# Routing weights also scattered to a table in DRAM, from GpSimd, inside an encoder kernel

## The reference

```python
q = (xc @ wq).reshape(C, PEER_HEADS, 2, half)                 # 8 heads, two halves of 128
s = jnp.einsum('thpd,hpkd->thpk', q, subkeys)                 # 128 keys a side
sv, si = lax.top_k(s, PEER_TOPK)                              # 16 best of each side
cand = sv[:, :, 0, :, None] + sv[:, :, 1, None, :]            # 16 x 16 sums
cid = si[:, :, 0, :, None] * PEER_NKEYS + si[:, :, 1, None, :]
fs, fi = lax.top_k(cand, PEER_TOPK)                           # 16 experts a head
g = jax.nn.softmax(fs, axis=-1)
a = jax.nn.gelu(jnp.einsum('tc,thkc->thk', xc, u_tab[eid]))
out = jnp.einsum('thk,thkc->tc', g * a, v_tab[eid])
```

## Time and profile before

| | |
|---|---|
| timed runs | 2017.39, 2022.19 and 2021.06 us, median 2021.06 |
| profiled execution | span 2017.2 us; the page gives no other time for it |
| TensorE busy | 2008.9 us (100% of the span), granted clock 0.9 to 1.0 of full in all slices |
| GpSimd (POOL) busy | 1603.3 us (79%) |
| VectorE (DVE) busy | 1298.3 us (64%) |
| ScalarE (ACT) busy | 1118.2 us (55%) |
| DMA | 358.41 MB, 178 GB/s on average |

### The profile page before, as it was taken

One profiled execution on the slowest core, in us unless ns is written; L12 is line 12 of the kernel. 1 busy time (PEld: TensorE's weight loads), 2 busy tenths in 40 slices (PEclk: granted clock), 3 DMA queues, 4 the chain that ended last, 5 costly groups with the idle time before them and its releaser, 6 DMA issues.

```text
span 2017.2 us, 42413 instructions
## 1 busy us (share of the span) xinstructions
PE 2008.9 (100%) x12436; PEld 1745.7 (87%) x12436; DVE 1298.3 (64%) x2815; ACT 1118.2 (55%) x2453; POOL 1603.3 (79%) x1316
## 2 busy tenths in 40 slices
PE   9999999999999999999999999999999999999999
PEld 8989888888888888888888898888888888888887
DVE  6787599888887333333378865998888873333333
ACT  6565666654444555555565556556544455555554
POOL 7777879987777888888877677998877778888886
PEclk9999999999999999999999999999999999999999
DMA  9444645544444555555584455555544445555554
GB/s 278 166 145 147 209 162 190 187 169 148 154 146 147 196 190 195 194 191 194 191 244 151 135 178 177 178 185 180 167 155 147 153 149 197 189 196 190 195 193 150
DMA packets 103396, 358.41 MB, mean 178 GB/s; under 512 B 11744, under 2 KB 16802, under 8 KB 103076
## 3 DMA queue, kind: packets, MB, share of 16 engines
q1 hardware_dynamic: 102900, 355.41, 53.0%
q10 hardware_dynamic: 432, 2.18, 0.3%
HBM read 356.49 MB, written 1.05 MB: 177 GB/s over the span
## 4 chain that ended last, share of the span: by engine, by line
PE 71%; POOL 15%; issue 11%; POOLq 0%; ACT 0%; DMA 0%; SPq 0%; DVE 0%; DVEq 0%; ACTq 0%
PE bank L1975 34%; PE bank L1621 21%; POOL w_lo L438 15%; PE bank L1623 10%; PE bank L1914 4%; PE bank L1594 0%; PE bank L1598 0%; PE bank L1596 0%; PE bank L1893 0%; DMA ring<-stream 0%; POOLq L436 0%; POOLq L459 0%; ACT w_hi L501 0%; SPq L403 0%; PE bank L2001 0%
## 5 line engine op out<-in xcount | busy, mean ns | idle before, releaser
L438 POOL TENSOR_TENSOR w_lo<-ring,w_hi 128x512 fp32r<-128x512 f32 x1048 | 1401.4, 1353 | 323.6 <-ACT w_hi L501 322.7
L501 ACT ACTIVATE w_hi<-ring 128x512 fp32r<-128x512 f32 x1312 | 752.5, 620 | 185.4 <-PE bank L1598 131.6
L1621 PE MATMUL bank<-act_parts,w_hi 128*128 128x512 f32 x2048 | 722.8, 398 | 0.4 <-POOL w_lo L438 0.2
L1623 PE MATMUL bank<-act_parts,w_lo 128*128 128x256 f32 x2048 | 569.8, 278 | 0.0
L438 DVE TENSOR_TENSOR w_lo<-ring,w_hi 128x512 fp32r<-128x512 f32 x256 | 236.7, 925 | 450.0 <-ACT w_hi L501 449.8
L1621 PEld LDWEIGHTS bank<-act_parts,w_hi 128*128 128x128 f32 x2048 | 384.2, 188 | 88.9 <-POOL w_lo L438 0.9
L1975 PE MATMUL bank<-w_hi,e_hi 128*128 128x512 f32 x1024 | 398.9, 390 | 0.2
L1975 PE MATMUL bank<-w_hi,e_lo 128*128 128x512 f32 x1024 | 398.4, 389 | 0.0
L1975 PE MATMUL bank<-w_lo,e_hi 128*128 128x512 f32 x1024 | 398.4, 389 | 0.0
L1623 PEld LDWEIGHTS bank<-act_parts,w_lo 128*128 128x128 f32 x2048 | 385.4, 188 | 0.0
L837 ACT ACTIVATE e_hi<-arena 128x256 fp32r (+1 forms) x256 | 106.8, 418 | 316.0 <-PE bank L1975 316.0
(11 more groups left out here) (245 smaller groups left out, 2533.2 us busy)
## 6 DMA issues: line engine op xcount, KB each, us to landing
ring<-stream SPq DMA_DIRECT2D x654, 512.0 KB, 3.3
arena<-rpb_in SPq DMA_DIRECT2D x8, 512.0 KB, 7.3
arena<-dft_in SPq DMA_DIRECT2D x4, 512.0 KB, 5.0
arena<-subkeys ACTq DMA_DIRECT2D x2, 1024.0 KB, 5.7
ring<-stream SPq DMA_DIRECT2D x4, 256.0 KB, 5.4
xT<-x_in SPq DMA_DIRECT2D x4, 256.0 KB, 5.6
arena<-w_in SPq DMA_DIRECT2D x2, 512.0 KB
arena<-decay_in SPq DMA_DIRECT2D x2, 512.0 KB
```

The lines of the kernel that those rows point to most:

```text
L438: eng.tensor_tensor(w_lo[:, part_, :], ring[:, tile % RING, half * HT:(half + 1) * HT], w_hi[:, part_, :].bitcast(F32), ALU.subtract).then ...
L501: nc.scalar.activation(w_hi[:, 2 * (tile % AHEAD) + half, :], ring[:, tile % RING, half * HT:(half + 1) * HT], ACT.Copy).then_inc(hi_ready ...
L1621: T.matmul(out_[:, 0:2 * S], weights(w_hi, tile, k), both[:, :, k, :], start=(k == 0), stop=False, skip_group_check=True)
L1623: ins = T.matmul(out_[:, 0:S], weights(w_lo, tile, k), both[:, 0, k, :], start=False, stop=(k == KT - 1), skip_group_check=True)
```

## The change

Only the second layer is touched. VectorE, right after `route_done`, computes for the first 128 tokens the place of each slot's weight in a table (token + 256 x (i + 128 x j), by the code below), and copies the weights to a tile of their own; then it signals `places_made`. GpSimd's loop of that layer ends at tile 163. Its last 36 tiles below 200 (164 to 199, which are u_tab's tiles 92 to 127) are written out one by one, and behind the low halves of each even one an indirect DMA writes one slot: 128 weights of 4 bytes, one per partition, each to its own place in a table of 16.8 MB in DRAM. These are 18 DMAs, of slots 0 to 17. GpSimd waits for `places_made` before tile 164, and for the 18 landings at the end of the program. Nothing reads the table. (The constant SPREAD_TILES is not used.)

```diff
+SPREAD_AT = 92
+        token_col = sb("token_col", [P, 1])
+        place_u = sb("place_u", [P, PH * TOPK], U32)
+        weight_u = sb("weight_u", [P, PH * TOPK])
+        weights_out = nc.dram_tensor("weights_out", (NK * NK * S, 1), F32, kind="Internal").ap()
...
-                with pool.Fori(1, POOL_TILES // RING) as i:
+                first_turns = POOL_TILES // RING if l == 0 else (T_U + SPREAD_AT) // RING
+                with pool.Fori(1, first_turns) as i:
                     for s in range(RING):
                         low_parts(pool, l, i, s)
+                if l:
+                    pool.wait_ge(places_made, 1)
+                    for n in range(T_U + SPREAD_AT, POOL_TILES):
+                        low_parts(pool, l, 0, n)
+                        if n % 2 == 0:
+                            slot = (n - T_U - SPREAD_AT) // 2
+                            pool.indirect_dma_start(
+                                weights_out, bass.IndirectOffsetOnAxis(ap=place_u[:, slot:slot + 1], axis=0),
+                                weight_u[:, slot:slot + 1], None).then_inc(spread_out, 16)
...
             for l in range(DEPTH):
                 pool_layer(l)
+            pool.wait_ge(spread_out, 16 * ((NK - SPREAD_AT) // 2))
...
+                def spread_places():
+
+                    flat = top_if[:, :, :, :].rearrange("p a b c -> p (a b c)")[:, 0:PH * TOPK]
+                    rest_ps = bank[6][:, 3 * P:4 * P]
+                    link(V.tensor_tensor(rest_ps, identity, iota[:, :], ALU.mult))
+                    link(V.tensor_reduce(token_col[:, :], rest_ps, AX, ALU.add))
+                    link(V.scalar_tensor_tensor(flat, slots[:, 0, 1, :], float(NK), slots[:, 0, 0, :],
+                                                ALU.mult, ALU.add))
+                    link(V.tensor_scalar(flat, flat, float(S), token_col[:, 0:1], ALU.mult, ALU.add))
+                    V.tensor_copy(weight_u[:, :], slots[:, 0, 2, :])
+                    V.tensor_copy(place_u[:, :], flat).then_inc(places_made, 1)
...
                 V.drain().then_inc(route_done.sem, 1)
+                if l:
+                    spread_places()
                 worked(80, ROUTED)
```

More of the change, by code:

```diff
@@ L61 @@
 LATE = NK - ROUTED
+SPREAD_AT = 92
+SPREAD_TILES = 32
 C_G1, C_G2, C_GB, C_QG, C_KG, C_CW, C_CB = 0, 8, 16, 32, 33, 34, 70
@@ L320, in encoder_kernel @@
         route_done = sig("route_done", 1)
+        places_made = sem("places_made")
+        spread_out = sem("spread_out")
         onehot_j_made = sig("onehot_j_made", TGROUPS)
```

## The result

Over 18 executions each on the same chip the kernel before took 2020.93 us (2017.39 to 2025.05) and the changed one 2028.88 us (2024.51 to 2030.55). The ratio is 1.0039, 95% interval 1.0033 to 1.0045: 6.7 to 9.1 us more. The forecast was 2026. The time lies in its range, also just inside the narrow one of the likeliest case (2020 to 2029), but the class with most chance (within 0.3%) did not come: the change costs 0.39%.

The account below looks back on a forecast made before the run. TensorE was taken to bound the kernel. VectorE's lateness (4.0 us) plus the last DMA (1.1) made 5.1 us on the median of 2021.06, so 2026 us (+0.25%), range 2019 to 2045.

Parts of the forecast that it names:

- the likeliest case: Whole kernel: DMAs hidden, VectorE's lateness costs TensorE 4 us; chance 0.50, taken alone 2020 to 2029 us.
- the class with most chance: Whole kernel: time within 0.3% of the kernel before (6.1 us, up to 2027.1); chance 0.51.
- TensorE bounds, and the DMAs are hidden by GpSimd's rest: Layer 2's late tiles: 17 DMAs of 1.3 us each cost nothing; two-tile turns stay at TensorE's 7.00 us.
- The room of 1.9 us a turn: Layer 2's late tiles: GpSimd rests 0.23 + 1.68 us per two-tile turn, so a DMA up to 1.9 fits.
- Rival A: Layer 2's late tiles: a DMA holds GpSimd over 1.9 us, making it the bound; 2038 to 2124 us, chance 0.28.
- The last DMA costs 1.1: Behind tile 126, GpSimd runs without rest, so the last DMA delays TensorE by 1.1 us.
- VectorE's instructions wait for the end of GpSimd's instruction: Behind route_done: VectorE's six new instructions with SBUF operands wait for GpSimd's halves; the next sum starts 4.8 us late.
- rival B: Behind route_done: VectorE's waits don't bite, sum 2.9 us late, TensorE loses 2.1; 2024 us, chance 0.12.
- TensorE loses 4.0 of it: First late tiles of layer 2: VectorE's 4.8 us lateness less 0.8 of room costs TensorE 4.0 us, once.
- the room was 1.1, not 0.8: Before the 24 small matmuls near 1440: group 3's one-hots were put 0.83 us ahead of TensorE's need.
- Packets: Layer 2's stream: 2304 small packets must triple a ring refill's 3.2 us landing before ScalarE waits; no cost.
- Code loading (C): First DMA on GpSimd loads code: 0.7 us more, 2027 us, or 5.4 more, 2031.5, by the skill; chance 0.07.

Follow-up runs that it names:

- e7: Changed kernel with new tensors last, places computed in VectorE's earlier rest, weights copied by ScalarE, DMAs behind tiles 88 to 122: 2016.73 us, 0.9998.
- e6: Changed kernel with new tensors last and VectorE's six new instructions replaced by eight, none with both sides in SBUF: 2020.32 us, 1.0012.
- e5: Changed kernel with its three new SBUF tensors allocated behind all others, so no old one moves: 2021.21 us, 1.0019.
- e4: Kernel before with the three new SBUF tensors allocated ahead of the one-hots (shifted 1028 bytes), used by nobody: 2023.47 us, 1.0027.
- e10: Kernel before with unused place_u and weight_u in front of the one-hots (shifted 1024 bytes): 2020.47 us, 0.9999.
- e11: Kernel before with unused token_col alone in front of the one-hots (shifted 4 bytes): 2025.21 us, 1.0030.
- e1: Changed kernel without the DMAs and with GpSimd's loop as before; VectorE's six instructions and the three tensors stay: 2028.43 us, 1.0052.
- e8: Changed kernel with tensors last, places and weights from constants, two DMAs behind each even tile (36): 2027.98 us, 1.0044.
- e9: Changed kernel with tensors last, places and weights from constants, three DMAs behind each even tile (54): 2052.92 us, 1.0171.
- e0: Kernel before, with no edit, timed against itself and profiled a second time: 2019.80 us, 1.0005.

## Why the prediction was right or wrong

- **TensorE bounds, and the DMAs are hidden by GpSimd's rest**: right. The turn of layer 2's late stretch is 7.00 us with them. One DMA was put at 1.3 us; with its rest it is 1.15. The room of 1.9 us a turn is confirmed from the other side: 1.15 fits and 2.43 lengthens the turn by 0.46. Rival A (0.28) did not occur; 0.75 us more on each DMA would have made it true.
- **The last DMA costs 1.1**: 0.9 measured, seen as idle in front of tile 127 in all kernels that have it there, and gone in e7.
- **VectorE's instructions wait for the end of GpSimd's instruction**: right, and rival B wrong. Waiting were the place (0.94 us), the scaling by 256 (1.36) and the copy of the weights (1.23); the casting and the reduction were short, as forecast. So three were at 0.8 us or more, where four were forecast. The first product took only 0.48 because it started 0.34 before GpSimd's half ended. In sum 4.5 late, forecast 4.8. With one side in PSUM the same lengths are 0.28 to 0.34 (e6). The Trainium skill's page "SBUF — State Buffer", section "Who interferes with whom", gives two SBUF inputs and the two-port modes as what locks; the rows agree, the copy with a single input included.
- **TensorE loses 4.0 of it**: 3.4 measured, or 2.9 if only what the rows show is counted. The step was right in kind and in place (between 1430 and 1441, behind ScalarE's gelus L844 and L868, which stand behind VectorE's late sums); the room was 1.1, not 0.8. e5 shows this step and the one before alone: +3.8 us, forecast 5.1.
- **Packets**: the 2304 small packets of the prediction are 576 by the profile, and the stream's tiles land in 3.3 us as before.
- **Code loading (C)**: the first DMA took 1.10 us, 0.12 more than the others. It did not occur; the 6 us of the Trainium skill's "GPSIMD Engine Reference", section "Instruction dispatch", are not seen here.
- **The step that failed** is one that was not in the sum: the change was taken to touch the second layer only, and the three tensors that it declares got no term and no reason why they should cost nothing. Three SBUF tensors of 1028 bytes a partition, placed in front of the one-hots, lengthen each pair of late matmuls in layer 1 by 7 ns: +3.1 us, 40% of what was measured. e4 shows it without any new instruction, e5 takes it away from the changed kernel, e10 and e11 put it on the 4 bytes. Without it the change would be at 1.0019 and inside the class forecast.
- **Where the number was lucky**: the mechanisms that were forecast cost 3.8 us by e5, not 5.1, and the placement, which was not forecast, made the total 7.9. That 2028.88 still lies in the narrow range is owed to the width of that range, which reached to 2029 for other reasons.

Why 4 bytes matter stays open. The one-hots and weighted_j shift by them, and VectorE writes them and TensorE reads them as bf16 in these turns; what meets what wasn't tried. Also open is why the changed kernel and e1, alone among the kernels with this shift, have the fast pace in layer 2's late stretch; both enter it behind TensorE's rests of 0.5 to 1.2 us. Both profiles are also of the fastest execution of their kernel, and no profile of another execution was taken, so their slower ones may have the slow pace there.

## What to carry to other kernels

When a change moves the time by tenths of a per cent, first compare a stretch that it doesn't touch: if that moved too, the cause is one that the diff's instructions don't show, such as where tensors lie. Put new small tensors behind the hot ones, or keep the old addresses. Work given to an engine that has rests still needs a place: the order in e7 costs nothing that these runs can tell, and the same work behind route_done and on tile 126 costs 4 us (e5). PSUM operands alone halve VectorE's lateness, from 4.5 to 2.3 us (e6).

## What the runs showed of the hardware

**Two paces of the same matmuls.** In most stretches of u_tab tiles the pair of matmuls is about 347 or about 353 ns long on average, at a granted clock of 1.00 in both. In layer 1's late stretch it follows where the tensors lie in all 14 profiled kernels: 353 to 354 in the six where the one-hots are shifted by 1028 or 4 bytes, 347 in the eight others. In layer 2's late stretch e8 and e9, whose turns wait for GpSimd, drift between the two (347 to 352 in pieces of 20 us), which I can't explain. The piece of 20 us between the copy of the weights and the first routing of layer 2 is slow in 10 of the 14, e0 and e10 among them, and fast in before, the changed kernel, e1 and e5. In the earlier stretches it changes from one kernel to another with no edit near it: the row of the high-part matmul between 1260 and 1425 us, first before, then after:

```profile
L1621 PE MATMUL bank<-act_parts,w_hi x465: 391/398/505, 1259.9 to 1424.8; 128*128 128x512 f32 x155
```

```profile
L1654 PE MATMUL bank<-act_parts,w_hi x472: 391/392/497, 1260.1 to 1425.0; 128*128 128x512 f32 x158
```

This is the -2.5 of the account: there the profiled execution of before had the slow pace and that of after the fast one. The unchanged kernel of e0 has the fast pace there and the slow one in layer 1, the reverse of before: one program has both. Each such stretch is worth about 3 us, which is a good part of the scatter of the kernel before (2017.4 to 2025.1), so a profile of one execution is compared stretch by stretch. That these switches make up the scatter is an inference; only profiled executions show the pace.

**An indirect DMA of 128 single words** holds GpSimd 0.98 us, 1.1 to 1.3 with the rest before it, and counts 32 packets (576 for 18). Tripling them left the landing of the stream's tiles at 3.3 us.
